# Expert routing of a fused transformer program: the block table built pair by pair behind its operands, one barrier of all engines taken out, and two changes to the order of weight loads

## The reference, cut to what matters

```python
def hier_moe(xf, w_rg, b_rg, w_re, b_re, w1, w3, w2):
    ...
    expert = g_idx * EXPERTS_PER_GROUP + top_i          # two experts for every token
    ...
    counts = jnp.bincount(e_flat, length=N_EXPERTS)
    padded = (counts + MOE_BLOCK - 1) // MOE_BLOCK * MOE_BLOCK
    pad_end = jnp.cumsum(padded)
    ...
    row_tok = jnp.full((R,), T, jnp.int32).at[dest].set(t_flat[order])
    block_exp = jnp.clip(jnp.searchsorted(pad_end, ...), 0, N_EXPERTS - 1)
    xb = x_pad[row_tok].reshape(n_blocks, MOE_BLOCK, D)

    def expert_block(args):
        xblk, e = args
        return (jax.nn.silu(xblk @ w1[e]) * (xblk @ w3[e])) @ w2[e]

    yb = lax.map(expert_block, (xb, block_exp)).reshape(R, D)
    out = jnp.zeros((T + 1, D), yb.dtype).at[row_tok].add(yb * row_gate[:, None])
    return out[:T]
```

## Time and profile before

| | |
|---|---|
| median of 3 runs | 3084.39 us (3083.84 to 3085.94) |
| the profiled execution | 3084.61 us, of which the span from first to last instruction is 3082.8 us |
| busy, share of the span | PE 90%, PEld 59%, DVE 42%, ACT 26%, POOL 9% |
| mean granted TensorE clock | 0.946 of full speed |
| blocks of layer 0 | from 1620 us to about 2130 us |
| blocks of layer 1 | from 2558 us to about 3053 us |

### The profile page before, as it was taken

The page is one execution under the profiler, slowest core; times in us unless marked ns, Lnnn a source line. Parts: engine busy times, 40 slices in busy tenths (PEclk is TensorE's granted clock), DMA queues, the critical chain, the costliest instruction groups (busy, mean ns, idle before and its releaser), DMA issues. The chain is left out here.

```text
span 3082.8 us, 34488 instructions
## 1 busy us (share of the span) xinstructions
PE 2763.1 (90%) x12578; PEld 1809.7 (59%) x12578; DVE 1293.5 (42%) x2007; ACT 805.2 (26%) x1339; POOL 270.0 (9%) x390
## 2 busy tenths in 40 slices
PE   7999989999989999799959988886888978998886
PEld 5888867766767888587833433333655543433333
DVE  5776685555457675603241110112556641111012
ACT  3223235454343232322220000001326620000000
POOL 0111100000001111021100111110000000111110
PEclk9999999999999999899979999998898988999997
DMA  5565521211225666311078999988110058999997
GB/s 207 212 220 219 211 89 69 70 68 69 103 88 185 219 220 237 137 68 41 28 288 360 422 387 393 404 346 331 47 43 1 1 234 349 421 370 399 401 401 286
DMA packets 116868, 666.06 MB, mean 216 GB/s; under 512 B 16158, under 2 KB 20638, under 8 KB 52128
## 3 DMA queue, kind: packets, MB, share of 16 engines
q1 hardware_dynamic: 77024, 536.35, 44.4%
q0 software_dynamic: 33408, 104.90, 9.7%
q10 hardware_dynamic: 6336, 23.50, 2.1%
HBM read 685.38 MB, written 24.38 MB: 230 GB/s over the span
## 5 line engine op out<-in xcount | busy, mean ns | idle before, releaser
L917 PE MATMUL bank<-big 128*64 128x512 f32 x784 | 361.8, 608 | 67.4 <-DMA big<-in_w 65.3
L2256 DVE TENSOR_TENSOR big<-big,bank 64x512 f32<-64x512 f32 x65 | 45.0, 692 | 845.0 <-ACT big L1504 845.0
L920 PE MATMUL bank<-big 128*64 128x512 f32 x848 | 392.0, 608 | 0.0
L917 PEld LDWEIGHTS bank<-big 128*64 128x64 f32 x784 | 105.2, 140 | 299.0 <-issue 297.0
L932 PE MATMUL bank<-big 128*64 128x512 f32 x912 | 243.5, 683 | 29.5 <-DVE big L2260 29.5
L1927 DVE SCALAR_TENSOR_TENSOR tabs<-tabs,tmp 128x1024 f32<-128x1024 f32 x160 | 193.6, 1223 | 178.4 <-DMA tabs<-in_wm 177.8
L1357 ACT ACTIVATE w_high<-slot 128x1024 fp32r<-128x1024 f32 (+1 forms) x138 | 140.8, 1041 | 205.2 <-DMA slot<-in_w 103.3
L2673 POOL DMA_DIRECT2D tabs<-in_wm x160 | 85.0, 532 | 1164.4 <-DVE tabs L1927 724.4
L607 PE MATMUL bank<-u_split,w_low 128*128 128x512 f32 x720 | 177.8, 389 | 0.0
L1504 ACT ACTIVATE big<-bank 64x512 f32<-64x512 f32 x65 | 38.3, 589 | 491.9 <-PE bank L917 491.9
L932 PEld LDWEIGHTS bank<-big 128*64 128x64 f32 x912 | 68.8, 155 | 161.7 <-issue 124.4
(11 more groups left out here) (408 smaller groups left out, 5323.3 us busy)
## 6 DMA issues: line engine op xcount, KB each, us to landing
big<-in_w SPq DMA_DIRECT2D x330, 1024.0 KB, 16.1
slot<-in_w SPq DMA_DIRECT2D x120, 1024.0 KB, 4.8
tabs<-in_wm POOLq DMA_DIRECT2D x160, 512.0 KB, 4.8
ar_u<-in_w SPq DMA_DIRECT2D x24, 1024.0 KB, 14.6
slot<-in_wd SPq DMA_DIRECT2D x16, 1408.0 KB, 6.6
ar_f<-in_w SPq DMA_DIRECT2D x20, 1024.0 KB
tabs<-in_w SPq DMA_DIRECT2D x10, 1024.0 KB
tmp<-in_w SPq DMA_DIRECT2D x10, 1024.0 KB
```

The lines of the kernel that those rows point to most:

```text
L917: ga = nc.tensor.matmul(bank[0][lo, :], xT[:, 4 * c + k, :], w1[:, k * EF:(k + 1) * EF], **flags)
L920: mm = nc.tensor.matmul(bank[0][hi, :], xT[:, 4 * c + k, :], w3[:, k * EF:(k + 1) * EF], **flags)
L2256: nc.vector.tensor_tensor(hmul[MB:2 * MB, :], hsil[MB:2 * MB, :], bank[0][MB:2 * MB, :], ALU.mult).then_inc(q["h_ready"], 1)
```

## The change

It does five things.

1. **Pairs.** `in_block` and `at_place` are built in turns, and each pair increments the semaphore `routed`; PE waits for each pair before its product (`placed(l, n)`), in place of one wait for all of them. The small product of the list of experts (`cmp`) moves from ahead of the last tiles' rows to behind the first pair's product.
2. **DVE's order.** The copy of the ranks stands ahead of the wait for `starts`; `exp_i` is written behind all pairs, where it stood ahead of the ranks. Four multiplications and four sums over 192 elements become two and two over 384 (layer 1: 128 and 256).
3. **Rows.** `EARLY_ROWS` is 4 and not 3, with a fourth row buffer that lies where `at_place` comes later, so DVE waits for the copy of the fifth tile (layer 1: for the DMA of the fourth) before it builds the pairs.
4. **Barrier.** PE, DVE, ACT and POOL wait for `expert` in place of the `phase.end()` ahead of the loop.
5. **SP.** Of layer 0's first twelve pieces seven are issued earlier (three at `xc_ready`, four at `dft_full`); of layer 1's second six, two are issued earlier (at `o_evac`). The third set's last two pieces wait for the first gather's landing (`gathered`) beside `table`.

```diff
-        EARLY_ROWS = 3
+        EARLY_ROWS = 4
...
                 if l == 0:
+                    sp.wait_ge(xc_ready, 2 * KT + 4)
+                    for c in ORDER[3:]:
+                        load(c, NE - 1)
+                    sp.wait_ge(dft_full, 4)
+                    for c in ORDER[1:2] + ORDER[3:]:
+                        load(c, NE - 2, 1)
                     sp.wait_ge(full[3], R_EO + 4)
+                    for c in ORDER[:3]:
+                        load(c, NE - 1)
+                    for c in (0, 1):
+                        load(c, NE - 2, 1)
                 else:
                     sp.wait_ge(o_full, 2 * (UNITS // 4))
-                for c in ORDER:
-                    load(c, NE - 1)
-                if l == 1:
+                    for c in ORDER:
+                        load(c, NE - 1)
+                    sp.wait_ge(o_evac, 2 * (UNITS // 4))
+                    for c in (4, 5):
+                        load(c, NE - 2, 1)
                     sp.wait_ge(full[3], R_WO + 2)
-                for c in ORDER:
-                    load(c, NE - 2, 1)
+                    for c in ORDER[:4]:
+                        load(c, NE - 2, 1)
                 sp.wait_ge(q["expert"], l + 1)
...
                 sp.wait_ge(q["table"], l + 1)
+                sp.wait_ge(q["gathered"], 16)
                 for c in ORDER[4:]:
                     load(c, e2, 2)
...
-                pe.wait_ge(q["routed"], routed(l, "tab_in"))
-                for x in range(2 * nt):
-                    mm = nc.tensor.matmul(bank[2][:, 0:TABW], at_place[:, x, :], in_block[:, x, :],
-                                          start=(x == 0), stop=(x == 2 * nt - 1))
+                for n in range(2 * nt):
+                    pe.wait_ge(q["routed"], placed(l, n + 1))
+                    mm = nc.tensor.matmul(bank[2][:, 0:TABW], at_place[:, n, :], in_block[:, n, :], start=(n == 0), stop=(n == 2 * nt - 1))
+                    if n == 0:
+                        nc.tensor.matmul(bank[6][0:2, 64:64 + TABW], ones[0:NE, 0:2], cmpb[0:NE, 0:TABW], start=True,
+                                         stop=True).then_inc(q["route_sums"], 1)
...
-                phase.end()
+                pe.wait_ge(q["expert"], l + 1)
                 last = pe.value_load(exp_i[0:1, TABW:TABW + 1], min_val=rotated + 3, max_val=NBMAX - 1)
...
+                dve.wait_ge(q["xt_cp"], TT * l + min(nt, EARLY_ROWS + 1))
+                if nt == EARLY_ROWS:
+                    dve.wait_ge(q["xt_out"], 16 * (TT * l + nt))
+                for t in range(nt):
+                    for x in range(2):
+                        nc.vector.tensor_scalar(in_block[:, 2 * t + x, :], ..., ALU.is_equal, ALU.mult)
+                        nc.vector.tensor_scalar(at_place[:, 2 * t + x, :]..., ..., ALU.is_equal).then_inc(q["routed"], 1)
```

More of the change, by code:

```diff
@@ L278, in program @@
         yrows = [[part((2 * t + x) * D, [D]) for x in range(2)] for t in range(TT)]
-        row_bufs = [xg] + [part(third_at + n * D, [D]) for n in range(2)]
+        row_bufs = [xg] + [part(third_at + n * D, [D]) for n in range(2)] + [part(m0 + D, [D])]
         rt = third_at + 2 * D
@@ L287, in program @@
         oh = [part(rt + 648 + 192 * n, [TT, NE]) for n in range(2)]
+        choices = part(rt + 648, [2, TT, NE])
         both = part(rt + 1032, [TT, NE])
+        picked = part(rt + 1032, [2, TT, NE])
         rank = part(rt + 1224, [TT, NE])
@@ L1510, in copy_y @@
                     nc.scalar.activation(ysb, bank[4][:, :], ACT.Copy).then_inc(q["y_ready"], 1)
-                phase.end()
+                act.wait_ge(q["expert"], l + 1)
                 last = act.value_load(exp_i[0:1, TABW:TABW + 1], min_val=2, max_val=NBMAX - 1)
@@ L2209, in moe_layer @@
                 nc.vector.tensor_copy(ovv, ovi)
-                dve.drain()
+                dve.wait_ge(q["route_sums"], route_sum(l, "starts"))
                 nc.vector.tensor_copy(nbb[:, 0:NE], bank[5][:, 0:NE])
+                nc.vector.tensor_copy(col[0:NE, 2:3], bank[6][0:NE, 0:1])
                 dve.drain()
@@ L2260, in copy_h @@
                     nc.vector.tensor_copy(hT, bank[6][:, 0:EF // P * MB]).then_inc(q["ht_ready"], 1)
-                phase.end()
+                dve.wait_ge(q["expert"], l + 1)
                 last = dve.value_load(exp_i[0:1, TABW:TABW + 1], min_val=2, max_val=NBMAX - 1)
@@ L2645, in moe_layer @@
                 gather_pair(0)
-                phase.end()
+                pool.wait_ge(q["expert"], l + 1)
                 last = pool.value_load(exp_i[0:1, TABW:TABW + 1], min_val=rotated + 3, max_val=NBMAX - 1)
```

39 lines of the change are left out of this document (17 added, 22 removed).

## The result

The changed kernel took 3065.99 us, median of 4 runs (3061.86 to 3066.70), the kernel before 3084.11 (3083.69 to 3085.94): ratio 0.9937, 95% interval 0.9925 to 0.9950. It is 18 us faster. The forecast was 3073.0 with a range from 3069.5 to 3079.5; direction right, size too small by 7 us, outside the range. A second set of 5 runs of the same kernel gave 3063.47, ratio 0.9932 (0.9918 to 0.9946). The profiled execution took 3065.89 us, its span 3064.1.

What follows compares the result with a forecast made beforehand. The prediction took DMA transfers in the loop over blocks to bound the kernel. Gains of 6.6 us in layer 0 and 4.8 in layer 1 summed to 11.4, giving 3073.0 us as a median, range 3069.5 to 3079.5.

Steps and rivals of the forecast that it cites:

- DVE's order, pairs, product: Layer 0's routing: earlier ranks, wider operations and product pair by pair start POOL's gather at 1603.3 instead of 1610.40.
- the product did not lag: Rival, chance 0.20: each table product on PE waits for its own pair, up to 0.87 us a product; 3079.0.
- Layer 1's chain: Layer 1's routing: fourth tile costs 1.4 us, earlier `wr` load gives 0.7; net 2.1, POOL's gather 2.33 later at 2543.6.
- Landing takes 8.9 (layer 1: 8.7): From the start of POOL's first gather to its landing: 8.9 us in layer 0, 8.7 in layer 1.
- It is not behind them in a line: The gather's packets run beside the weight pieces, so holding back two pieces of the third set gains nothing.
- Barrier, 0.8 a layer: Ahead of the loop over blocks: removing the barrier saves 0.8 us a layer, bounds 0 and 0.9.
- The later of the two decides: A layer's end moves with R or D, whichever is later; gains 6.6 us in layer 0, 4.8 in layer 1.
- The DMA engines are what never rests: Loop over blocks: DMA share 1.00 to 1.01 at about 400 GB/s, so a layer ends when the transfers end.
- R: Restart of packets when block 0 gives back its first buffer: 1629.6 and 2567.9 before, forecast 1621.6 and 2562.2.
- D: End of the third set's transfers, forecast 1623.0 in layer 0 and 2563.1 in layer 1.
- the expert list: Rival, chance 0.04: `exp_i` written behind all pairs holds the third set, slower, 3089.6 were a pair 1.25 us.
- blocks, not transfers: Rival, chance 0.08: PE's first block decides, the third set's lateness does not matter; gain 8.0 + 5.7 = 13.7, 3070.7.

Runs made afterwards that it cites:

- e5: The kernel before with only the barrier ahead of the loop over blocks taken out, engines waiting for the expert list instead: 3079.84 us, ratio 0.9986.
- e2: The changed kernel with the expert list written ahead of the pairs again, so the third set's loads start earlier: 3069.35 us, ratio 0.9958.
- e4: The kernel before with one wait more: SP loads the third set only once the first gather has landed: 3077.05 us, ratio 0.9978.
- e7: The changed kernel with PE waiting once for all pairs in place of one wait for each: 3077.18 us, ratio 0.9977.
- e1: The changed kernel without SP's wait for the first gather ahead of the third set's last two pieces: 3065.98 us, ratio 0.9942.
- e3: The changed kernel with the barrier of all four engines ahead of the loop put back: 3065.63 us, ratio 0.9939.
- e9: The changed kernel with the early expert list; third set's pieces behind the gather, except three of layer 0 issued at once: 3062.50 us, ratio 0.9929.

## Why the prediction was wrong in size

- **DVE's order, pairs, product: right.** From the router's copy to POOL's gather 36.1 us became 29.1, 7.1 less, as forecast (1610.4 to 1603.3). Operations over 384 elements took 0.56 (0.57 taken), pairs 0.42 with an increment on each, products 0.45: the product did not lag, and its end came 1.3 us behind the last pair. The increments cost nothing: a pair takes 0.42 before, without one, and after, with one. The Trainium skill's "the semaphore costs nothing extra here" (VectorE: DVE Perf Modes, "The DRAIN you can't avoid") is borne out.
- **Layer 1's chain: right, but for `wr`.** PE still waited for `wr` until 2.1 us behind ACT's start, as before, so the 0.7 did not come; the fourth tile ahead of the second exponential cost 1.5 (20.4 us from PE's first router product to DVE's first step behind the exponential became 21.9), forecast 1.4. POOL's gather is 4.0 us earlier behind that first product, against a net forecast of 4.2 without `wr`.
- **"Landing takes 8.9 (layer 1: 8.7)": wrong, the first of two failed steps.** It took 4.2 and 3.4. As a number for a gather beside weights without the barrier it was nearly right (e5: 8.54 and 8.58). The forecast read the number off a gather that ran beside weights, and carried it over to one that does not. It had the times that say so: `exp_i` behind the pairs puts the loads at 1605.6, and the gather at 1603.3. e2, e4 and e7 show it both ways.
- **"It is not behind them in a line": half right.** Once there, the gather's packets do run beside the weights, as the earlier trace rows show. But in the kernel before the first one came 4.6 and 4.2 us behind POOL's start and not 1.8. The rule of the Trainium skill that the forecast leaned on (DMA: Bandwidth & Descriptors, "SWDGE vs HWDGE vs iDMA": a DMA engine takes the two kinds of queue in turn) agrees with the first and says nothing of the second. The figure of the Trainium skill for the first byte of a software queue, about 1 us (DMA: Bandwidth & Descriptors, "Latency and other measured facts"), is below even the 1.7 to 1.8 that the quiet runs show from POOL's start. The forecast gave the two held-back pieces nothing, and e1 shows that to be right, for another reason: the late list already does what the hold is written for.
- **Barrier, 0.8 a layer: right as an interval** (0.7 to 1.2 in e3 and e5); as a time only e5 shows something.
- **"The later of the two decides", layer 0: right.** Block 0 came 13.1 us earlier behind the router's copy and the last block 7.1 (mean of five profiles), forecast 6.6, by the third set. That the two numbers are so close is in part luck: the five profiles lie between 5.6 and 9.3.
- **The same in layer 1: wrong, the second failed step.** "The DMA engines are what never rests" was read from stretches that left out 2567.9 to 2766. There stood the 6.4 us stop. A restart R at 2567.9 was thus not on the line that ends the layer, and D was set against it though that line had 6.4 us in hand: D, later than R by only 0.9 in the forecast, could cost nothing, and the layer had to follow its first product. Block 0 came 10.2 us earlier, the layer ended 10.0 earlier, forecast 4.8.
- **Neither error alone would have shown.** With the right landing and the forecast's rule, D still decides both layers, and the sum stays at 11.4. With the right rule and a landing of 8.7, layer 1 gains the 5.7 of its first product, less the 0.7 of `wr`, 5.0. Together, 5.7 + 5.3 (8.7 to 3.4) - 0.7 = 10.3, and 10.0 was measured. 7.1 and 10.0 are 17.1 of the 18.1 and 20.3 that the two comparisons show; the other 1 to 3 us are not placed: executions of one kernel differ by as much, and they stay open.
- **Rivals.** The product did not lag; the expert list was at 1598.6 and not late; "blocks, not transfers" was true of layer 1, and its price was too low because it kept the old landing.

## What to carry to other kernels

A gather's latency in a profile belongs to the traffic beside it: before it is carried over, look up which transfers are under way when it starts in the new order, and if it stands on the critical path, let bulk loads start behind it (one line did this for the old kernel and gave 7 us). The same holds for the small write that such a gather waits for. Before a stretch is called bound by transfers, look for short stops of the DMA engines in all of it, above all where buffering changes: here a stop with PE fully busy went with transfers that had time in hand. Where two lines meet, price a change on each of them, since a gain on one is cut by the other (layer 0 kept 7 of 13 us, layer 1 all 10).

## What the hardware showed that was not expected

- An indirect DMA's first packet came 1.7 to 1.8 us behind POOL's start on idle queues, 4.1 to 4.6 us with weight pieces running on another queue, although both then run side by side. Why the start and not only the transfer is held is not settled by these runs: no experiment parts the making of the gather's descriptors from their way to the engines.
- With weights throughout, the first gather (144 packets, 0.2 to 0.4 MB) took 8.2 to 9.8 us to reach PE (7.0 in layer 0 of e2, where two pieces were held back); when the weights stopped 3.8 us behind POOL's start it took 4.7 (its first packet came at 2.9), and when they stopped at 3.0 it took 4.5 (first packet at 2.5).
- A write of 0.5 MB issued 0.1 us behind three weight pieces took 7.2 us to land (e2, e9), in place of 2.6 without them.
- POOL's drain ends with the landing of its indirect DMA, not with its issue: before, the issue ended at 1611.5, the gather's last packet at 1618.8, and the barrier let go at 1619.3. With the barrier PE began 0.7 to 1.2 us later than without, in quiet and in loaded queues alike.
